# A transformer block and a retention, Fourier and convolution block: the order of the first tiles and weight slices, the norms' root, the norms in front of the feed-forward part by pairs, and an end by tiles

## The chip, the cores and the metric

One core of a Trainium2 chip runs the whole program, in one launch, float32 in and out. The metric is the device time in microseconds, the median of several executions; an execution's profile adds a span (first to last instruction of the program) and the clock granted to TensorE. The engines are PE (TensorE; PEld is its loading of stationary tiles), DVE (VectorE), ACT (ScalarE), POOL (GpSimd) and SP (SyncE, which here only issues DMAs).

## The reference

Two blocks follow each other on x (1024 tokens of width 1024). The first has two layers of attention over 16 meta tokens and the sequence, in 8 groups of two heads; the second one layer with a token mixer and a feed-forward part:

```python
for l in range(2):                               # first block
    proj = rmsnorm(h, norm_gain[l]) @ w_in[l]    # q, k, v, gates, forget
    ...
    h = h + concat(do, fo) @ w_out[l]
x = rmsnorm(h, final_gain)[:, 16:]
h_lat = modulate(rms_norm(x, g_mix_pre), sh_a, sc_a)          # second block
mix = token_mixer(h_lat, w_in, w_out, ...)       # retention | Fourier
x = x + gt_a * rms_norm(mix, g_mix_post)
h_ffn = modulate(rms_norm(x, g_ffn_pre), sh_f, sc_f)
u = conv3(h_ffn @ w_up)                          # 2 * 2816 columns
x = x + gt_f * rms_norm((silu(u_a) * u_b) @ w_down, g_ffn_post)
```

Every rms norm is x / sqrt(mean(x * x) + 1e-6) over a row.

## The kernel before

**Products.** A matrix product is three matmuls (`mm3`, L559): each operand is split into a high part rounded to fp32r and the rest, AH and AL for activations, WH and WL for weights, and high*high, high*low and low*high are added up in PSUM, a bank of 512 columns each. The activations of a stage stand transposed in AH and AL, 8 tiles of 128 rows. Weights come in slices of 512 KB: SP loads slice w into one of two slots of W32 (L2328) once the slice two before it is split; ACT writes WH (L1103) once PE is done with the slice two before (`W_OVER`); DVE writes WL (L1567). `split_to(w)` does all slices up to w at that place of an engine's program.

**Order.** Each engine has one program in order, written out by hand; counting semaphores (`mark` and `at`) tie them together. PSUM banks are planned ahead: `banks.take` gives the bank that was taken longest ago and names what its user before has to have finished, and PE waits for that.

**A norm** works on pairs of token tiles (`PAIRS`; the fifth has the 16 meta rows; for the first block `PAIR_ORDER` begins with it). ACT squares each tile with a sum into a column (L1115), DVE scales the sums by 1/1024 and adds 1e-6 (`mean`, L1573), ACT takes Ln (L1117) and Exp of -0.5 times it (L1119), DVE multiplies the tiles by it (L1602; L1883 between the blocks; L2132 in front of the feed-forward part), PE transposes them (L568, 16 transposes a pair over 8 banks), and the result is written to AH and AL: in the first block by ACT (L1150) and DVE (L1610); between the blocks by ACT into one of two buffers (L1337), POOL into AH (L2288) and DVE into AL (L1889); in front of the feed-forward part, 512 columns at a time, by ACT (L1134) and DVE twice (L1589, L1591).

**Start.** SP loads constants, the meta rows, then the 8 tiles of x with the first two weight slices behind the fourth and the sixth (L2330 to L2341). ACT's order is: statistics of the meta rows, of pair 0, fill of the meta rows, statistics of pair 1, fill of pair 0, statistics of pair 2, splits of the slices for q and k, fill of pair 1, statistics of pair 3. PE then does chunks of the first projection (352 or 344 tokens, 24 matmuls): q 0, fill of pair 2, k 0, fill of pair 3, q 1, q 2, k 1, k 2.

**Between the blocks** each pair of the last layer is added (L1840), normed by the final gain (L1875, stored to xs by POOL), normed once more and filled, while PE begins the context's product, whose 512-column results ACT evicts (L1354).

**In front of the feed-forward part.** The product `out2` runs in quarters of 256 columns: for the first three all tiles with the first weight slice and then the second, in the last pair by pair. ACT (L1461) and DVE (L2119) evict two pairs each into MX. When all are there, for four tiles at a time: squares, root, product with the root and the gate row GA (L2125), add of XL (L2128), squares again, root, scaling (L2132). XL has room for four tiles; POOL reloads each when its add is done (L2309) and stores the sum to xs (L2310). Then all is transposed and filled, and only when the last fill is done does the up projection begin: 22 blocks of 128 columns, for each the halves a and b, for each two chunks of 512 tokens, with a convolution on ACT (L1485) and DVE (L2149, L2152) behind each.

**End.** The down projection runs in two halves of 512 columns, for each k of 22 all eight tiles (eight banks). ACT (L1513) and DVE (L2176) evict. Behind the last matmul DVE makes the gate row (L2068), and four tiles at a time ACT squares both halves (L1522, L1523), takes Ln and Exp (L1526, L1528), DVE multiplies (L2189) and adds (L2192), and POOL stores each tile (L2320); SP waits for the stores.

## Time and profile before

| what | value |
|---|---|
| time, median of 3 runs | 3196.71 us (3195.51 to 3205.25) |
| profiled execution | 3192.36 us, span 3190.6 us |
| mean granted clock of TensorE | 0.952 of 2.4 GHz |
| busy PE, DVE, ACT, POOL | 2850.3, 1543.7, 1058.5, 170.3 us |
| moved by DMA | 198.06 MB, mean 62 GB/s |

A row of a group of instructions has its line, engine, operation, what it writes and reads with the shapes, the count, then busy time, mean ns of one, and the idle time of the engine ahead of them with what ended it. A window's row has the busy time of each engine in that stretch (number of instructions in brackets) and the granted clock as a share: 1.00 is 2.4 GHz, 0.50 is 1.2 GHz. In a timeline the first two numbers are start and duration; brackets hold idle time ahead and the releaser.

### The profile page before, as it was taken

The numbers are of one execution on the slowest core, as the hardware profiler recorded it, in microseconds if no ns is written. First come the engines' busy times: TensorE is split into PE (matmuls) and PEld (weight loads), VectorE is DVE, ScalarE is ACT, GpSimd is POOL, SyncE is SP. The second block draws the span as 40 slices with busy tenths as digits, with TensorE's granted clock in tenths as the row PEclk, the third lists the DMA queues.
The fourth block names the chain that finished last, engine by engine and source line by source line (L and its number), as shares of the span: only waits on it lengthen the run. The fifth ranks groups of instructions, "written<-read, shape, count | busy, mean of one in ns | idle before, by whom it ended". The sixth has DMA issues, their size and how long they took to land.

```text
span 3190.6 us, 42795 instructions
## 1 busy us (share of the span) xinstructions
PE 2850.3 (89%) x17412; PEld 2434.0 (76%) x17412; DVE 1543.7 (48%) x2759; ACT 1058.5 (33%) x1867; POOL 170.3 (5%) x263
## 2 busy tenths in 40 slices
PE   5889999999789899999997969999948999999994
PEld 5777777887778777787886857888937888887883
DVE  4555654545335555555454355553244444444334
ACT  6333333333143233332233371223243222223222
POOL 1000000000001011000001020000000000000000
PEclk9899999999899999999998879999979999999997
DMA  5212221211321221222213131112221111111121
GB/s 121 39 52 60 62 54 55 62 41 41 114 86 31 50 62 56 54 65 65 59 47 112 39 123 36 40 53 98 73 93 41 47 47 47 52 47 40 53 104 62
DMA packets 205393, 198.06 MB, mean 62 GB/s; under 512 B 7286, under 2 KB 181686, under 8 KB 205198
## 3 DMA queue, kind: packets, MB, share of 16 engines
q1 hardware_dynamic: 186192, 130.07, 15.8%
q0 software_dynamic: 19008, 65.26, 5.5%
q8 instruction: 140, 2.29, 0.3%
q14 instruction: 53, 0.43, 0.0%
HBM read 162.73 MB, written 32.58 MB: 61 GB/s over the span
## 4 chain that ended last, share of the span: by engine, by line
PE 77%; DVE 9%; ACT 6%; issue 4%; DMA 3%; POOL 0%; SPq 0%; ACTq 0%; DVEq 0%; POOLq 0%
PE PS L559 73%; PE PS L568 4%; DMA W<-in_w_in 2%; DVE WL L1567 1%; DVE ST L1744 1%; ACT WH L1103 1%; ACT top L1242 1%; DMA TMP<-s_os 1%; ACT L1117 1%; DVE AL L1610 1%; ACT OTt L1115 0%; ACT R L1115 0%; DVE AL L1591 0%; DVE V L1732 0%; DVE R L2189 0%
## 5 line engine op out<-in xcount | busy, mean ns | idle before, releaser
L559 PE MATMUL PS<-AH,WH 128*128 128x344 f32 (+2 forms) x2608 | 991.6, 380 | 37.0 <-DVE AL L1610 21.4
L559 PE MATMUL PS<-AL,WH 128*128 128x344 f32 (+2 forms) x2608 | 921.0, 353 | 0.0
L559 PE MATMUL PS<-AH,WL 128*128 128x344 f32 (+2 forms) x2608 | 918.4, 352 | 0.0
L559 PEld LDWEIGHTS PS<-AH,WH 128*128 128x128 f32 x2608 | 498.0, 191 | 120.0 <-DVE AL L1610 23.0
L559 PEld LDWEIGHTS PS<-AL,WH 128*128 128x128 f32 x2608 | 499.0, 191 | 50.5 <-issue 1.4
L559 PEld LDWEIGHTS PS<-AH,WL 128*128 128x128 f32 x2608 | 497.0, 191 | 44.0
L1567 DVE TENSOR_TENSOR WL<-W,WH 128x1024 fp32r<-128x1024 f32 x188 | 230.0, 1226 | 398.6 <-ACT WH L1103 398.2
L559 PE MATMUL PS<-WH,AH 128*128 128x256 f32 (+1 forms) x1152 | 369.4, 321 | 15.1 <-DVE AL L2171 7.2
L559 PE MATMUL PS<-WL,AH 128*128 128x256 f32 (+1 forms) x1152 | 368.1, 320 | 0.0
L559 PE MATMUL PS<-WH,AL 128*128 128x256 f32 (+1 forms) x1152 | 368.0, 319 | 0.0
L1103 ACT ACTIVATE WH<-W 128x1024 fp32r<-128x1024 f32 x188 | 197.3, 1051 | 348.8 <-PE PS L559 322.8
L1744 DVE TENSOR_REDUCE ST<-PS 128x1 f32<-128x784 f32 (+8 forms) x272 | 188.0, 732 | 150.4 <-PE PS L559 150.0
L568 PE MATMUL PS<-ident,top 128*128 128x128 f32 (+2 forms) x1132 | 190.1, 284 | 71.9 <-issue 20.6
L559 PEld LDWEIGHTS PS<-WH,AH 128*128 128x128 f32 x1152 | 222.1, 193 | 33.3 <-DVE AL L2171 7.7
L559 PEld LDWEIGHTS PS<-WH,AL 128*128 128x128 f32 x1152 | 222.1, 193 | 15.3
L559 PEld LDWEIGHTS PS<-WL,AH 128*128 128x128 f32 x1152 | 221.9, 193 | 15.2
L1242 ACT ACTIVATE top<-PS,ST 128x784 f32<-128x784 f32 (+8 forms) x272 | 194.2, 721 | 90.4 <-DVE ST L1744 58.2
L568 PEld LDWEIGHTS PS<-ident,top 128*128 128x128 f32 (+2 forms) x1132 | 134.0, 136 | 106.3 <-issue 42.1
L559 PE MATMUL PS<-top,V 128*64 128x256 f32 (+6 forms) x1176 | 185.7, 378 | 19.9 <-DVE top L1781 17.1
L559 PEld LDWEIGHTS PS<-top,V 128*64 128x64 f32 (+3 forms) x1176 | 120.5, 156 | 88.0 <-issue 43.4
L1485 ACT ACTIVATE R<-PS,R 128x512 f32<-128x512 f32 x88 | 68.6, 780 | 321.4 <-PE PS L559 321.4
L2149 DVE SCALAR_TENSOR_TENSOR R<-PS,R 128x504 f32<-128x504 f32 x88 | 65.4, 743 | 208.7 <-ACT R L1485 208.7
(300 smaller groups left out, 3163.9 us busy)
## 6 DMA issues: line engine op xcount, KB each, us to landing
W<-in_w_in SPq DMA_DIRECT2D x94, 512.0 KB, 7.4
W<-in_w_ada SPq DMA_DIRECT2D x48, 512.0 KB, 3.6
W<-in_w_up SPq DMA_DIRECT2D x44, 512.0 KB, 3.7
W<-in_w_out SPq DMA_DIRECT2D x24, 512.0 KB, 3.4
W<-in_w_down SPq DMA_DIRECT2D x22, 512.0 KB, 3.6
R<-s_xs POOLq DMA_DIRECT2D x16, 512.0 KB, 6.0
s_adap<-AST POOLq DMA_DIRECT2D x48, 128.0 KB, 7.4
top<-in_x SPq DMA_DIRECT2D x8, 512.0 KB, 9.6
```

The costliest lines, as they stand in the source:

```text
L559: return e.matmul(out, lhsT, rhs, start=start, stop=stop, skip_group_check=True)
L568: return e.transpose(out, in_, ident[0:k, 0:k])
L1103: e.activation(WH[:, t, :], W32[:, s, :], ACT.Copy).then_inc(*w_hi.mark(v))
L1117: e.activation(cols[0:r, :], cols[0:r, :], ACT.Ln).then_inc(*logged.mark(tag))
L1242: e.activation(P[0:rows, P_SLOT[u], 0:W], PSf[0:rows, o:o + W], ACT.Exp, bias=st[:, 0:1], accum_out=st[:, 1:2]).then_inc(*exped.mark(u))
L1485: e.activation(dst[:, c:c + n], bank(b), ACT.Identity, scale=CW[:, 1, jj:jj + 1], bias=CW[:, 3, jj:jj + 1]).then_inc(*conv_a.mark((j, ab, ...
L1567: e.tensor_tensor(WL[:, t, :], W32[:, s, :], f(WH[:, t, :]), ALU.subtract).then_inc(*w_lo.mark(v))
L1610: e.scalar_tensor_tensor(lo, bank(b)[:, 0:n], COLS[:, 8 * l + k:8 * l + k + 1], f(hi), ALU.mult, ALU.subtract).then_inc(*fill_lo.mark((l, ...
L1744: e.tensor_reduce(ST[0:rows, ST_SLOT[u], 0:1], PSf[0:rows, o:o + W], AX.X, ALU.max, negate=True).then_inc(*row_max.mark(u))
L2149: e.scalar_tensor_tensor(d3[:, :, 1:64], o3[:, :, 0:63], CW[:, 0, jj:jj + 1], d3[:, :, 1:64], ALU.mult, ALU.add).then_inc(*conv_v.mark((j, ...
```

## The change

- **Root.** `mean`, Ln and Exp become ACT's Sqrt with scale 1/1024 and a bias column EPS, and DVE's reciprocal, in all norms but that of the retention.
- **Start.** For the first layer ACT and DVE do: statistics of the meta rows, of pair 0, fill, statistics of pair 1, fill, split of q's slice, fill of pair 1, statistics of pair 2, split of k's slice. PE's chunks are q 0, fill of pair 2 (then statistics of pair 3 on ACT and DVE), k 0, q 1, fill of pair 3, k 1, q 2, k 2; the constants' set-up stands ahead of q 2.
- **In front of the feed-forward part.** Each quarter of `out2` is squared by ACT from PSUM, 256 columns at a time into SQ, and written to MX by DVE already multiplied by the gate row. Root, add and second norm go by pairs, the first two beside the last quarter. The fill of pair 0 stands on PE between the third and the fourth pair of that quarter, that of pair 1 behind it, those of pairs 2 and 3 between the first chunks of the up projection, which for the first block goes a 0, b 0, a 1, b 1. ACT fills 256 columns into one of four buffers, POOL writes AH, DVE AL.
- **End.** In the second half the last four k go tile by tile. ACT squares the first half during the second, and DVE multiplies it by the gate row, made ahead; of each tile of the second half the bank itself is squared and multiplied, one root a tile, one product with the root and add over 1024 columns. SP issues the stores.
- **Besides.** The load of the convolution's constants stands ahead of the Fourier part; stores of two tiles share a semaphore.

The diff, cut to its core:

```diff
@@ statistics (ACT) and its DVE part
-                e.wait_ge(*mean_sq.at(tag))
-                e.activation(cols[0:r, :], cols[0:r, :], ACT.Ln).then_inc(*logged.mark(tag))
-                e.wait_ge(*logged.at(tag))
-                e.activation(cols[0:r, :], cols[0:r, :], ACT.Exp, scale=-0.5).then_inc(*rstd.mark(tag))
+                e.wait_ge(*squared.at((tag, len(tiles) - 1)))
+                e.activation(cols[0:r, :], cols[0:r, :], ACT.Sqrt, scale=1.0 / D, bias=EPS[0:r, :]).then_inc(*root.mark(tag))
...
-                e.tensor_scalar(cols[0:r, :], cols[0:r, :], 1.0 / D, 1e-6, ALU.mult, ALU.add).then_inc(*mean_sq.mark(tag))
+                e.wait_ge(*root.at(tag))
+                e.reciprocal(cols[0:r, :], cols[0:r, :]).then_inc(*rstd.mark(tag))
@@ scalar(e), norm
+                if l == 0:
+                    norm_stats(0, 4)
+                    norm_stats(0, 0)
+                    norm_fill(0, 4)
+                    norm_stats(0, 1)
+                    norm_fill(0, 0)
+                    split_to(WI[0, 0, "q"])
+                    norm_fill(0, 1)
+                    norm_stats(0, 2)
+                    split_to(WI[0, 0, "k"])
+                    return
@@ tensor_fourier and tensor_ffn
-            tensor_out(e, "out2", [128 * t for t in range(8)], first, lambda q, p: (mix_act if p % 2 else mix_dve, (q, p)))
+            tensor_out(e, "out2", [128 * t for t in range(8)], first, lambda q, p: (mix_dve, (q, p)),
+                       after=lambda i, among: tensor_norm_fill(e, "ffn", 0, among) if i == 2 else None)
+            tensor_norm_fill(e, "ffn", 1)
...
+                for ab, ci in UP_ORDER[j]:
+                    c, n = CH2[ci]
+                    if j == 0 and ab == 0:
+                        e.wait_ge(*fill_lo.at(("ffn", 2 * ci + 1, 7)))
+                    tensor_chunk(e, WI["up", j, ab], ("up", j, ab, ci), c, n, [(conv_v, (j, ab, ci))], ALL, ci == 1)
+                    if j == 0 and ci == 0:
+                        tensor_norm_fill(e, "ffn", 2 + ab, [b for b in ALL if b != banks.place["up", 0, ab, 0]])
...
+                together = FT - 4 * half
+                for k in range(together):
+                    for t in range(8):
+                        product(t, k)
+                for t in range(8):
+                    for k in range(together, FT):
+                        product(t, k)
@@ scalar(e), behind out2 (DVE: sum, add and scale of a pair at the same places)
+                mix_squares(3, 0)
+                mix_root(0)
+                sum_stats(0)
+                mix_squares(3, 1)
+                mix_root(1)
+                mix_squares(3, 2)
+                sum_stats(1)
+                mix_root(2)
+                ffn_fill(0)
+                mix_squares(3, 3)
+                split_to(WI["up", 0, 0])
+                ffn_fill(1)
+                split_to(WI["up", 0, 1])
+                sum_stats(2)
+                mix_root(3)
+                sum_stats(3)
+                ffn_fill(2)
@@ vector(e), the end
+                for t in range(8):
+                    r = RSTD[:, t:t + 1]
+                    e.wait_ge(*end_sq.at((t, 1)))
+                    e.tensor_tensor(r, r, RSTD[:, 8 + t:9 + t], ALU.add).then_inc(*end_v.mark(("sum", t)))
+                    e.tensor_tensor(G[:, t, 512:1024], bank(banks.place.get(("down", 1, t), 0)), GAf[:, 512:1024], ALU.mult).then_inc(
+                        *end_v.mark(("second", t)))
+                    inverse(("end", t), r)
+                    e.wait_ge(*rstd.at(("end", t)))
+                    e.wait_ge(*end_v.at(("second", t)))
+                    e.wait_ge(*tile_in[t].at("res"))
+                    e.scalar_tensor_tensor(XLf[:, t, :], G[:, t, :], r, XLf[:, t, :], ALU.mult, ALU.add).then_inc(*end_v.mark(("add", t)))
```

## Rows read from the trace of the kernel before

**Rows 1.** Page of the kernel before, busy time (share of the span)
```profile
PE 2850.3 (89%) x17412; PEld 2434.0 (76%) x17412; DVE 1543.7 (48%) x2759; ACT 1058.5 (33%) x1867; POOL 170.3 (5%) x263
```

**Rows 2.** Waits of PE, whole span: us in total, times, longest
```profile
PE PS L568 <- DVE R L2132: 41.7, 6, 26.0
...
PE PS L559 <- ACT R L1337: 16.5, 4, 14.5
```

**Rows 3.** Windows: us; busy PE, PEld, DVE, ACT, POOL; clock; DMA share; GB/s
```profile
0.00:37.62 37.62, 8.20 (x40) 7.04 (x40) 16.40 (x39) 31.93 (x61) 1.44 (x6) 0.87 0.87 209
...
1841.00:1863.05 22.05, 3.82 (x19) 3.31 (x17) 10.05 (x14) 20.60 (x32) 3.08 (x6) 0.57 0.27 112
...
2243.20:2334.60 91.40, 91.32 (x769) 90.88 (x767) 18.87 (x23) 13.33 (x17) 2.08 (x4) 1.00 0.19 64
...
2334.60:2401.60 67.00, 14.77 (x65) 10.68 (x65) 44.59 (x63) 44.42 (x67) 6.34 (x12) 0.58 0.29 102
...
3146.90:3190.60 43.70, 0.00 (x0) 0.00 (x0) 23.56 (x38) 17.12 (x41) 4.26 (x8) 0.55 0.24 96
```

**Rows 4.** Timeline, first 40 us: start us, us, engine, line, operation
```profile
8.84 0.20 ACT L1117 ACTIVATE SM<-SM 16x1 f32<-16x1 f32 x1
...
27.70 1.28 ACT L1117 ACT_TABLE_LOAD   x1
...
29.22 1.28 ACT L1119 ACT_TABLE_LOAD   x1
...
34.35 3.22 DVE L1610 SCALAR_TENSOR_TENSOR AL<-PS,COLS,AH 128x256 fp32r<-128x256 f32 x8
...
37.62 0.66 PE L559 MATMUL PS<-AH,WH 128*128 128x352 f32 x1 [9.60 <-DVE AL L1610]
```

**Rows 5.** Line L2328 (loads of W), its issue at 7.6 us
```profile
DMA to landing us min/median/max: 21.9/21.9/21.9
```

**Rows 6.** Windows at a gap of PE, columns as in rows 3
```profile
920.70:923.80 3.10, 0.00 (x1) 0.01 (x1) 1.62 (x4) 2.42 (x8) 0.96 (x2) 0.78 0.65 260
...
922.50:929.30 6.80, 5.50 (x26) 5.47 (x27) 2.32 (x10) 4.54 (x11) 0.00 (x0) 0.50 0.28 109
```

**Rows 7.** Timeline, norm of the second layer (ACT)
```profile
933.20 0.20 ACT L1117 ACTIVATE SM<-SM 128x2 f32<-128x2 f32 x1 [5.07 <-DVE SM L1573]
```

**Rows 8.** Timeline, between the blocks (ACT, DVE)
```profile
1875.52 0.58 ACT L1354 ACTIVATE R<-PS 128x512 f32<-128x512 f32 x1
...
1861.72 2.55 DVE L1567 TENSOR_TENSOR WL<-W,WH 128x1024 fp32r<-128x1024 f32 x2
```

**Rows 9.** Groups, 2334.6 to 2401.6 us: count, busy us, mean ns, idle
```profile
L1115 ACT ACTIVATE R<-R 128x1024 f32<-128x1024 f32 x16 | 16.9, 1056 | 14.7 <-DVE R L2128 13.1 <-DVE R L2119 0.9
...
L2125 DVE SCALAR_TENSOR_TENSOR R<-R,SM 128x1024 f32<-128x1024 f32 x8 | 10.2, 1280 | 5.7 <-ACT SM L1119 5.7
...
L2132 DVE TENSOR_SCALAR R<-R,SM 128x1024 f32<-128x1024 f32 x8 | 5.5, 748 | 5.7 <-ACT SM L1119 5.7
```

**Rows 10.** Groups by form, 1841 to 1905 us
```profile
L1337 ACT ACTIVATE R<-PS,COLS,SM 128x256 f32<-128x256 f32 x29 | 15.5, 561 | 11.0 <-DVE AL L1889 11.0
```

**Rows 11.** Windows: transposes alone, then matmuls; columns as in rows 3
```profile
2366.30:2369.70 3.40, 1.43 (x13) 1.19 (x11) 2.08 (x2) 1.24 (x2) 0.00 (x0) 1.00 0.00 0
...
2401.60:2407.30 5.70, 5.70 (x14) 4.50 (x15) 1.23 (x1) 1.06 (x1) 0.55 (x1) 0.50 0.05 16
```

**Rows 12.** Timeline, last weight slice (ACT, DVE)
```profile
3124.77 1.06 ACT L1103 ACTIVATE WH<-W 128x1024 fp32r<-128x1024 f32 x1 [8.13 <-PE PS L559]
...
3127.01 1.22 DVE L2171 TENSOR_TENSOR AL<-R,AH 128x1024 fp32r<-128x1024 f32 x1
```

**Rows 13.** Groups, 3124.7 to 3190.6 us
```profile
L1522 ACT ACTIVATE R<-R 128x512 f32<-128x512 f32 x8 | 5.0, 628 | 1.5 <-DVE R L2068 0.9
```

**Rows 14.** DMA issues from 3150 us: KB each, us to landing
```profile
out<-R POOLq DMA_DIRECT2D x8, 512.0 KB, 2.9
```

**Rows 15.** Sequencers at the end: ns min/median/max, start us
```profile
L96 POOLq DRAIN  x1: 8466/8466/8466, 3181.9 to 3181.9; - x1
```

More of the change, by code:

```diff
@@ L530, in build @@
         out_mm, out_added = count("out_mm"), count("out_added")
-        tile_out = [count(f"tile_out{i}") for i in range(8)]
+        tile_out = [count(f"tile_out{i}") for i in range(4)]
         fg_in, xc_in, fg_mul = count("fg_in"), [count(f"xc_in{i}") for i in range(2)], count("fg_mul")
@@ new lines, in fourier, with mix_root, sum_stats @@
+                    for p in range(4 if q < 3 else 0):
+                        mix_squares(q, p)
+                def mix_root(p):
+                    e.wait_ge(*mix_v.at(("sum", p)))
+                    r = RSTD[:, 2 * p:2 * p + 2]
+                    e.activation(r, r, ACT.Sqrt, scale=1.0 / D, bias=EPS).then_inc(*root.mark(("mix", p)))
+                def sum_stats(p):
+                    statistics(("mix2", p), [MX[:, t, :] for t in PAIRS[p]], lambda i: [(mix_v, ("add", PAIRS[p][i]))], RSTD[:, 8 + 2 * p:10 + 2 * p], JF)
@@ new lines, in ffn @@
+                        if half and 1 <= k <= 8:
+                            t = k - 1
+                            e.wait_ge(*(down_act if t % 2 else down_dve).at(t))
+                            if t:
+                                e.wait_ge(*end_sq.at((t - 1, 0)))
+                            e.activation(Jf[:, 0:512], F_OUT[t], ACT.Square, accum_out=RSTD[:, t:t + 1]).then_inc(*end_sq.mark((t, 0)))
+                    if half == 0:
+                        for t in range(1, 8, 2):
+                            b = banks.place.get(("down", 0, t), 0)
+                            e.wait_ge(*down_mm.at((0, FT - 1, t)))
+                            e.activation(F_OUT[t], bank(b), ACT.Copy).then_inc(*down_act.mark(t))
@@ new lines, in ffn @@
+                for t in range(8):
+                    e.wait_ge(*down_mm.at((1, FT - 1, t)))
+                    if t:
+                        e.wait_ge(*end_sq.at((t - 1, 1)))
+                    e.activation(Jf[:, 512:1024], bank(banks.place.get(("down", 1, t), 0)), ACT.Square, accum_out=RSTD[:, 8 + t:9 + t]).then_inc(
+                        *end_sq.mark((t, 1)))
+                    e.wait_ge(*end_v.at(("sum", t)))
+                    r = RSTD[:, t:t + 1]
+                    e.activation(r, r, ACT.Sqrt, scale=1.0 / D, bias=EPS).then_inc(*root.mark(("end", t)))
```

369 lines of the change are left out of this document (204 added, 165 removed).

## The prediction, made before the changed kernel ran

> **What bounds the kernel now.** The page comes first: PE is busy 2850.3 of the span's 3190.6 us [rows 1], so a change that touches no matmul can win back at most the 340 us in which PE stands still. Then PE's waits [rows 2]: the longest single ones are 26.0 us for L2132 (tiles scaled in front of the feed-forward part) and 14.5 us between the blocks. Then windows by stage [rows 3], which show where the idle time lies: 29.4 us ahead of the first projection (8.20 busy of 37.62), 18.2 between the blocks, 52.2 in front of the feed-forward part, and all 43.7 us behind the last matmul, 143.5 together. In each, ACT and DVE are busy by turns: the stages are chains, and what leaves the chain leaves the span. The window from 2243.2 to 2334.6 shows the opposite, a stage that PE fills (91.32 of 91.40).
>
> **Root and reciprocal in place of Ln and Exp.** For each pair of tiles ACT loads a table for Ln and another for Exp, 1.28 us each [rows 4]. Square and Copy load none in between, so they need no table of their own. With Sqrt alone the table stays: a pair's link shrinks from two loads, two ACTIVATEs of 0.20 us [rows 7] and a DVE step before them to one ACTIVATE with a DVE reciprocal behind it. I take the reciprocal of a few columns at 0.2 us, like those small steps; its bounds are 0.1 and the 0.75 of a whole tile's step [rows 9]. A pair saves 2.7 us of ACT. The Trainium skill (ScalarE: Activation LUTs, "Table sets: the hidden batching unit") says that one set holds both exp and ln, and that sqrt is in another; by that rule the exchange would save no load and add some, and -112 below would be about -70. The rows show a load ahead of each of the two, so they decide.
>
> **Start, -12.4.** PE's first chunk waits for the fill of the second pair, 37.57 [rows 4]. Before, ACT reads the third pair's statistics ahead of the split and that fill; now they stand behind (5.4 us), and the three links that stay ahead are 2.7 shorter (the 16-row tile's 1.5). Counted through: the first Ln stood at 8.84 [rows 4], and Sqrt stands there now and ends at 9.0; two squares (1.06 each [rows 9], and 0.2 each to read the sum, taken like a small ACTIVATE) and the root end at 11.7; 16-row fill and second pair's root at 15.6; 3.0 us of fill, 18.6; split of q, 19.6; second fill, 22.5. DVE follows with a scaling, a fill of 3.22 [rows 4], a split of 1.2 and another fill, and ends at 25.1: -12.4. The chunk for k needs the second slice, issued at 7.6 and landing 21.9 us later [rows 5], at 29.5; split it is ready at 31.8, and the chunk is due at 34.5, 9.4 after the first as before. So this load is barely in time: 3 us later and each further one is paid. Bounds -8 and -14.
>
> **Second layer's norm, -6.** Sqrt no longer stands behind DVE's add of the next pair; ACT waited 5.07 us there [rows 7]. Three links from add to fill are 1.6 us shorter (one load and its ACTIVATE): 4.8. The first follows a PE gap of 3.1 us, after which the granted clock was 0.50 (1.2 GHz) for 6.8 us with 5.50 of work [rows 6]; with a gap of 1.5 it may stay at 2.4 GHz, which is worth 2.5, and I count half. Bounds -3 and -8.
>
> **Between the blocks, -18.3.** The product ends at 1841.2 and DVE's add of its last pair at 1841.9. Then DVE has two products of 1.28, two scalings of 0.75, two products of 1.28 [rows 9] and three reciprocals, 7.2, and ACT's statistics (2.65 a pair, not 5.3) are in time for each. So its split starts at 1849.1 in place of 1861.72 [rows 8]: I take -12.9, with the load of DVE's queue at the first add. Further on ACT sets the pace: the eviction at 1875.52 [rows 8] stands behind two table loads, as does the next slice's: 2.7, twice. Bounds -13 and -21.
>
> **In front of the feed-forward part, -40.6.** ACT's and DVE's work on the first three pairs slides under the last quarter of the product, where PE takes 5.7 us a pair (91.40 for 16) [rows 3], so pairs end at 2317.5, 2323.2, 2328.9. Squares of 256 columns and the product with the gate row, both straight from PSUM, are new forms: I take 0.6 with the read and 0.7 us, nearest to the 0.63 of 512 columns [rows 13]; bounds 0.4 and 1.3 [rows 9]. A pair's handling, 2 us, stays under its 2.8 of PE. First pair: added until 2323.3, root 2324.8, scaled 2326.4. Second: added 2330.4, root 2333.1. PE's in-order fill of the first pair starts at 2328.9, but its last transposes wait for a bank that ACT frees only behind the second pair's root, at 2333.9. So the fourth pair's product, part of it at half clock, ends at 2342.8, not 2334.6. Its handling holds a bank of the second fill until 2345.0; ACT's split and 8 fills of 0.56 [rows 10] and DVE's behind them end at 2350.2, where the first chunk starts; it takes 8.3 us (14 of 24 matmuls in 5.7 at 1.2 GHz [rows 11], the rest at 0.23). Beside it the third and fourth pairs are squared, added and scaled until 2360.7; third fill and second chunk end at 2366.0, the fourth fill on DVE at 2371.3. There the third chunk starts and loses 2.7 to the clock: it counts as from 2374.0. Before, it began at 2415.4, two chunks (8.3 and 5.6) behind 2401.6: -41.4. Against it, the slice for the second half of the last quarter is split behind two squares and an eviction: +0.8. Bounds: -47 with full clock, -30 with all at half.
>
> **Tail, -35.0.** In the last half the final four k go tile by tile, so seven of eight tiles finish under PE (12 matmuls of 0.23, 2.77 us a tile). A tile needs ACT 0.63 and two small steps [rows 13], DVE 0.2, 0.7, 0.2 and 1.28 [rows 9], 2.4: they keep up. Behind the last matmul: square 0.8, sum 0.2, product 0.7 (root beside it), reciprocal 0.2, last product 1.3, hops 0.3, store 3.5 (POOL's took 2.9 [rows 14], I add some for another queue), end 0.3: 7.3. New wait: the last slice can be split only when k 17 is through, at 3124.77; the fill behind it ends at 3128.2 [rows 12], 3.5 later, where PE in the new order wants it after 9 matmuls, 2.1: +1.4. POOL's DRAIN takes 8.47 us behind its last store [rows 15] and ends the span; with the stores on SP it can run early. Of 43.7 us 8.7 stay. Bounds -30, if a DRAIN still follows the end, and -37.
>
> **Covered.** Fewer semaphores; the load of the convolution's constants ahead of the Fourier part and the gate row's ahead of the end, three DMAs of POOL under stages that PE fills to 0.99 [rows 3]; uncovered they cost their issue, 2 us in all. Sqrt also brings a table load to four later places with Exp or Tanh, beside PE's matmuls; on the path they cost 5.
>
> **Sum.** -12.4 -6.0 -18.3 -40.6 -35.0 = -112.3. The profiled execution took 3192.4: 3080.1. The median shown, 3196.7, lies 4.3 above it, and its three runs spread by 10. I forecast 3083 for the median.
>
> **Rivals.** *The clock stays low.* Pauses of 2 to 3 us keep PE at 1.2 GHz through the norms and from 2334 to 2380: another 12 us, 3095. For it: 0.58 is that stage's mean clock now [rows 3]. Against: 2.4 GHz was granted in a window with transposes alone, and came 5.7 us into the matmuls [rows 11]. Chance 0.2. The Trainium skill (TensorE: Matmul & The Clock Gate, "Part 4: PE-mode transpose") says that transposes do not count as busy; by that rule the fills would hold the clock down, and 3095 is what it gives. The first window of rows 11 speaks against it. *Tables come back.* Were Square or Identity missing from Sqrt's table, each root would cost two loads again, and the change would not do what it says: start -7, norm -2, blocks -3, front -29, tail -24 (ACT 3.6 us a tile against PE's 2.8): 3128. Against: Square runs in Exp's table without a load. 0.06. *More overlap.* Full clock in every stage, a store of 3: 3070. 0.16. *Slower.* A denser kernel is granted less clock: each 1% of mean clock costs 28.5 us of busy PE, so from 4% on it passes the 112 gained, and 6% gives 3255. Rows 3 have 91 dense microseconds at 1.00 and low clock only in the patchy windows. 0.01.
>
> **Numbers.** The sum has 0.57, the rivals the rest. The range is 3064 to 3103: it takes in the clock's case and the fuller overlap and leaves out tables and slower. A measurement of this kernel can tell some 0.3%, 10 us, from no change. Faster 0.98, same 0.01, slower 0.01.
>
> **What would show it.** Right: the first chunk at 25 us; no table load from 12 to 40 us; the first chunk between the blocks 9 us behind the product, not 22; no PE gap over 4 us in front of the feed-forward part; the last store issued by SP 4 us behind the last matmul. Wrong: PE's k chunk waiting for the second slice, a table load at every root, a PE wait of over 3 us at the last slice.

## The result, and the profile after

The changed kernel takes 3099.7 us (median of 4 runs, 3097.1 to 3102.0), the kernel before 3198.1 in the same series: a ratio of 0.969 [0.967, 0.971], 98.4 us less. The forecast was 3083 with a range of 3064 to 3103: the time lies inside, near its upper end, 16.7 above the forecast.

The profiled execution took 3101.8 with a span of 3099.8, 90.8 less than the span of before. First the page's busy times of the changed kernel, which answer to [rows 1]:

```profile
PE 2859.0 (92%) x17412; PEld 2438.5 (79%) x17412; DVE 1538.9 (50%) x2768; ACT 1011.7 (33%) x1865; POOL 183.2 (6%) x287
```

PE has the same 17412 matmuls and 8.7 us more of busy time; what left the span is idle time, 340.3 then and 240.8 now. ACT lost 46.8 us: 39 table loads of 1.28 us fewer are 50, and its other work grew by 3.

Windows by stage of the changed kernel, columns as in [rows 3]: until the first chunk; the rest of the first projections; between the blocks, from the product's end to the first chunk; 87.5 us of the out-projection that ends in front of the feed-forward part; from the fourth pair's product to the first up chunk; its first four chunks; behind the last matmul.

```profile
0.00:25.06 25.06, 7.75 (x41) 5.82 (x41) 13.74 (x36) 19.27 (x45) 1.43 (x6) 0.99 0.94 204
25.06:67.79 42.73, 36.05 (x194) 33.62 (x195) 22.39 (x50) 19.65 (x43) 5.59 (x5) 0.89 0.36 92
1835.80:1842.73 6.93, 0.01 (x1) 0.03 (x1) 6.86 (x10) 4.42 (x9) 2.69 (x5) 0.84 0.52 214
2221.50:2309.00 87.50, 86.57 (x732) 86.13 (x730) 31.68 (x43) 28.78 (x79) 5.86 (x12) 1.00 0.28 91
2312.90:2326.86 13.96, 9.22 (x61) 8.64 (x61) 12.51 (x23) 9.41 (x19) 8.25 (x16) 0.74 0.48 175
2326.86:2371.46 44.60, 32.87 (x128) 26.20 (x129) 20.44 (x33) 18.61 (x34) 9.54 (x18) 0.79 0.10 36
3093.85:3099.80 5.95, 0.00 (x1) 0.00 (x0) 2.24 (x5) 0.98 (x3) 0.00 (x0) 0.73 0.44 176
```

Beside [rows 3] the reader sees three things. The pause between the blocks is 6.93 us and has DVE at work for 6.86 of them: one engine is left in that chain, where ACT filled 20.6 of 22.05 before. In the out-projection PE is still full (86.57 of 87.50, at clock 1.00) while ACT has 28.8 us of work and DVE 31.7, where they had 13.3 and 18.9: this is the norm that slid under the product. And the window of the four chunks has PE idle for 11.7 us at a clock of 0.79. The first of its two pauses was not foreseen.

To see where each microsecond went, the two traces are cut at the same matmul, counted from the start of each (the 41st is the first chunk's; where the order differs, both orders have done the same amount); stages in us:

| stage (ends at matmul no.) | before | after | difference | forecast |
|---|---|---|---|---|
| to the first chunk (41) | 37.62 | 25.06 | -12.6 | -12.4 |
| first projections (234) | 38.02 | 42.73 | +4.7 | 0 |
| attention, first layer (5001) | 754.5 | 756.3 | +1.8 | 0 |
| norm of the second layer (5881) | 122.3 | 117.4 | -4.9 | -6.0 |
| attention, second layer (10501) | 724.5 | 728.8 | +4.3 | 0 |
| between the blocks (11904) | 260.8 | 245.4 | -15.4 | -18.3 |
| second block (14013) | 376.7 | 377.1 | +0.4 | 0 |
| in front of the feed-forward part (14341) | 112.1 | 78.7 | -33.4 | -40.6 |
| feed-forward part to the last matmul (17412) | 719.9 | 722.0 | +2.1 | +1.4 |
| end | 44.1 | 6.4 | -37.7 | -36.4 |

They sum to -90.8 against -112.3. Three places hold the difference: the first projections, attention stretches whose code did not change, and the stage in front of the feed-forward part.

Timeline of the changed kernel's start: the one table load for the root, the first chunks for q and k, DVE's scaling of the last pair, the set-up's table load and the matmul behind it (in brackets the engine's idle time and what ended it).

```profile
7.84 1.28 ACT L1144 ACT_TABLE_LOAD   x1
...
25.06 0.66 PE L569 MATMUL PS<-AH,WH 128*128 128x352 f32 x1 [3.83 <-DVE AL L1681]
...
34.37 0.43 PE L569 MATMUL PS<-AH,WH 128*128 128x352 f32 x1 [2.10 <-DVE AL L1681]
...
36.81 2.10 DVE L1673 TENSOR_SCALAR top<-top,SM 128x1024 f32<-128x1024 f32 x2
...
55.62 1.28 ACT L1214 ACT_TABLE_LOAD   x1
...
61.51 0.83 PE L569 MATMUL PS<-TMP,rotm 128*128 128x344 f32 x2 [2.78 <-ACT TMP L1254]
```

The first chunk starts at 25.06 and the one for k at 34.37; 25.1 and 34.5 stood in the working. Then the load at 55.62, for the Exp of the set-up, keeps ACT from the eviction that the rope product waits for, and PE stands still for 2.78 us at 61.51.

The same view in front of the feed-forward part, with DVE's fill (L2254) and its second convolution step (L2275):

```profile
2326.86 0.79 PE L569 MATMUL PS<-AH,WH 128*128 128x512 f32 x1 [2.85 <-DVE AL L2254]
...
2336.82 4.12 DVE L2254 TENSOR_TENSOR AL<-R,AH 128x256 fp32r<-128x256 f32 x8 [0.29 <-POOL AH L2444]
...
2341.63 0.74 DVE L2275 SCALAR_TENSOR_TENSOR R<-PS,R 128x504 f32<-128x504 f32 x1
...
2342.43 0.79 PE L569 MATMUL PS<-AH,WH 128*128 128x512 f32 x1 [5.63 <-DVE R L2275]
...
2356.50 0.74 DVE L2275 SCALAR_TENSOR_TENSOR R<-PS,R 128x504 f32<-128x504 f32 x1
...
2357.35 0.77 PE L569 MATMUL PS<-AH,WH 128*128 128x512 f32 x1 [5.85 <-issue]
```

The first up chunk starts at 2326.86. The second one's weights and data are there, and yet it starts 5.63 us after the transposes in front of it, directly behind L2275 at 2341.63. That is the convolution of the first chunk, which reads the first chunk's bank: the bank taken is the one taken longest ago, and that is the first chunk's own. DVE's convolution in turn stands in its queue behind eight steps of the third fill. The third chunk waits in the same way for the second's convolution at 2356.50; its own fill was through at 2355.8, so there the bank costs 1.4 of the 5.85.

The end of the changed kernel: PE at the last slice of weights, then the work of the last tile behind the last matmul (3093.85), and the stores.

```profile
3072.38 0.47 PE L569 MATMUL PS<-WH,AH 128*128 128x512 f32 x1 [1.11 <-DVE WL L1638]
...
3093.89 0.60 ACT L1596 ACTIVATE R<-PS 128x512 f32<-128x512 f32 x1 [1.57 <-PE PS L569]
...
3094.69 0.69 DVE L2312 TENSOR_TENSOR R<-PS,R 128x512 f32<-128x512 f32 x1
...
3094.80 0.29 ACT L1600 ACTIVATE SM<-SM 128x1 f32<-128x1 f32 x1 [0.23 <-DVE SM L2311]
...
3095.29 0.15 DVE L1644 RECIPROCAL SM<-SM 128x1 f32<-128x1 f32 x1
...
3095.48 1.28 DVE L2318 SCALAR_TENSOR_TENSOR R<-R,SM 128x1024 f32<-128x1024 f32 x1
```

```profile
out<-R SPq DMA_DIRECT2D x7, 512.0 KB, 2.6
```

PE waits 1.11 us at the last slice. Behind the last matmul: square 0.6, sum, gate product 0.69, reciprocal 0.15, last product 1.28, store 2.6; 5.95 in all.

### The profile page after: what moved, and what is told of

Same layout as the page of the kernel before. It is cut to its first block, busy times and chain, and to the rows that moved or that the text cites. A ratio compares the mean times of both kernels' runs of the same rounds, so it can differ in the third digit from the quotient of the medians.

```text
span 3099.8 us, 42844 instructions
## 1 busy us (share of the span) xinstructions
PE 2859.0 (92%) x17412; PEld 2438.5 (79%) x17412; DVE 1538.9 (50%) x2768; ACT 1011.7 (33%) x1865; POOL 183.2 (6%) x287
## 3 DMA queue, kind: packets, MB, share of 16 engines
q1 hardware_dynamic: 187344, 134.27, 16.6%
## 4 chain that ended last, share of the span: by engine, by line
PE 79%; DVE 9%; ACT 5%; issue 4%; DMA 3%; POOL 0%; SPq 0%; ACTq 0%; DVEq 0%; POOLq 0%
PE PS L569 75%; PE PS L578 4%; DMA W<-in_w_in 2%; DVE ST L1825 1%; DVE WL L1638 1%; ACT WH L1130 1%; ACT top L1278 1%; DMA TMP<-s_os 1%; DVE AL L2254 0%; DVE AL L1681 0%; DVE V L1813 0%; DVE top L1841 0%; DVE top L1838 0%; DVE AL L1900 0%; ACT AH L1316 0%
## 5 line engine op out<-in xcount | busy, mean ns | idle before, releaser
L569 PE MATMUL PS<-WH,AH 128*128 128x256 f32 (+1 forms) x1152 | 370.6, 322 | 16.7 <-DVE WL L1638 7.3
L569 PEld LDWEIGHTS PS<-WH,AH 128*128 128x128 f32 x1152 | 223.0, 194 | 35.7 <-DVE AL L2294 8.2
L1278 ACT ACTIVATE top<-PS,ST 128x784 f32<-128x784 f32 (+8 forms) x272 | 194.2, 720 | 90.6 <-DVE ST L1825 58.3
```

Of the source, the lines that this page charges most:

```text
L569: return e.matmul(out, lhsT, rhs, start=start, stop=stop, skip_group_check=True)
L1278: e.activation(P[0:rows, P_SLOT[u], 0:W], PSf[0:rows, o:o + W], ACT.Exp, bias=st[:, 0:1], accum_out=st[:, 1:2]).then_inc(*exped.mark(u))
```

## Experiments

All are the changed kernel with the edit shown, unless said otherwise; "..." marks lines of an edit that are left out. "Stage" is one of the table above. The span of one profile has up to 10 us of noise of its own (after_again shows it), so a stage is compared where the edit acts, and the medians for the whole. The changed kernel's own median was 3099.7 at first and 3097.2 when it ran once more. The differences of medians below are counted from 3099.7 and are uncertain by these 2.5 us.

**banks_free.** The second chunk may not take the first's bank, nor the third the second's.

```diff
-                    tensor_chunk(e, WI["up", j, ab], ("up", j, ab, ci), c, n, [(conv_v, (j, ab, ci))], ALL, ci == 1)
+                    late = {(0, 0, 1, 0): (0, 0), (0, 0, 0, 1): (1, 0)}.get((0, j, ab, ci))
+                    among = [b for b in ALL if late is None or b != banks.place["up", 0, late[0], late[1]]]
+                    tensor_chunk(e, WI["up", j, ab], ("up", j, ab, ci), c, n, [(conv_v, (j, ab, ci))], among, ci == 1)
```

> The changed kernel with one difference: of the first four chunks of the feed-forward part, the second may not take the bank of the first, nor the third that of the second, so neither has to wait for a convolution that DVE does behind eight steps of a fill. Theory 'bank': the 5.63 us gap at 2336.80 and most of the 5.85 us gap at 2351.50 in the changed kernel are waits for those banks; the second chunk then starts straight behind the transposes of the third fill, 5.5 us earlier and at the 2.4 GHz clock (another 2.7), the third chunk still waits for the last fill on ACT and DVE but for no convolution behind it (1.4 less), and the first part of the down product starts 8 to 10 us earlier, near 2837 instead of 2846; in all -7 to -10 us. Rival 'data': the second chunk waits for its weights or for the fill on DVE as well; the gap shrinks by at most 1.5 us and the time stays within 2 us.

Measured 3090.2 (3088.3 to 3093.9), 0.967 [0.965, 0.968] of before. The stage in front of the feed-forward part went from 78.7 to 68.0 us. PE's rows of that run with a wait:

```profile
2324.54 0.80 PE L569 MATMUL PS<-AH,WH 128*128 128x512 f32 x1 [2.89 <-DVE AL L2256]
...
2346.14 0.50 PE L569 MATMUL PS<-AH,WH 128*128 128x512 f32 x1 [3.99 <-DVE AL L2256]
```

Between the first chunk and the third (no. 14293) there is no pause for a bank; the third chunk waits only for its fill (L2256 is the fill's line here). Theory "bank" holds: the two waits and the half clock behind the first cost 10.7 us of that stage by these two profiles. The other profiles give this size its bounds: the seven with the banks as changed have the stage at 77.4 to 78.7 us, the three with the banks free (both and stats_later too) at 68.0 to 69.0. So the cost is 8.5 to 10.7 us.

**fills_first.** All four pairs filled ahead of the first chunk, chunks in their old order; everything else in front of the feed-forward part as changed.

```diff
-            tensor_norm_fill(e, "ffn", 1)
+            for p in (1, 2, 3):
+                tensor_norm_fill(e, "ffn", p)
...
-                    if j == 0 and ci == 0:
-                        tensor_norm_fill(e, "ffn", 2 + ab, [b for b in ALL if b != banks.place["up", 0, ab, 0]])
...
-        UP_ORDER = [[(0, 0), (1, 0), (0, 1), (1, 1)] if j == 0 else [(0, 0), (0, 1), (1, 0), (1, 1)] for j in range(FT)]
+        UP_ORDER = [[(0, 0), (0, 1), (1, 0), (1, 1)] for j in range(FT)]
```

> The changed kernel without the mixing of chunks and fills: all four pairs are filled ahead of the first chunk of the feed-forward part, and the chunks go in their old order; pairs, squares from PSUM and roots stay. Theory 'the banks eat it': in the changed kernel the third chunk starts at 2357.35; with the fills first, the third pair's fill ends on DVE at 2341, the fourth's at 2345.5, the first chunk starts there, and the third at 2345.5 + 8.3 + 5.6 = 2359.4. So mixing is worth only 2 to 3 us as it stands, and 12 with the banks free. Rival 'the mixing is the gain': the time rises by 8 us or more.

Measured 3093.0 (3089.8 to 3093.4), 0.967 [0.965, 0.968]; the stage takes 70.3 us, 8.4 less than as changed. (ACT and DVE do the last fill ahead of their first convolution.) Both readings put down beforehand missed the sign. The rows of PE in that run show why:

```profile
2329.48 3.65 PE L578 MATMUL PS<-ident,R 128*128 128x128 f32 x16 [6.49 <-DVE R L2219]
...
2335.42 3.43 PE L578 MATMUL PS<-ident,R 128*128 128x128 f32 x16 [2.29 <-ACT R L1540]
...
2338.76 0.76 PE L569 MATMUL PS<-AH,WH 128*128 128x512 f32 x1
```

I had let the first chunk wait for the last fill on DVE. It needs only the first two pairs, so it starts straight behind PE's last transposes, at 2338.76, and its 6.5 us cover the rest of the last fill on ACT and DVE. From there PE has no pause. So of the 33.4 us gained in this stage none comes from mixing chunks and fills: that part costs 8.4 as it stands. With the banks free it is worth 1.4 to 2.3 by the stage (69.0 to 68.0 against 70.3), which the medians, 3093.0 and 3090.2 with overlapping ranges, cannot tell from nothing.

**exp_early.** One Exp of one column behind the last pair's root, where ACT is idle.

```diff
                 def step_stats(p):
                     norm_stats(l, p)
+                    e.activation(SM[:, 63:64], EPS, ACT.Exp)
```

> The changed kernel with one ACTIVATE more: an Exp of one column right behind the root of the last pair of tiles at 36.3 us, where ACT is idle until 40.0. Theory 'late table': of the 4.7 us that the start gives back between 46 and 62 us, 1.3 is the table load of the set-up's Exp at 55.62, and the rest the lower clock behind the longer pause of 2.78 us; with the load moved, that pause shrinks to 1.5 or less, the clock stays, and the start keeps 10.5 to 12 us at 62 us instead of 7.9: -2 to -4 us. Rival 'place': the set-up stands in ACT's queue ahead of the eviction whatever its table, 2.9 us of copies and small steps that stood two chunks later before; then at most 1.3 us comes back.

Measured 3097.1 (3091.8 to 3100.2), 0.969 [0.967, 0.970]. In the profile the load moved under ACT's idle time and PE's pause is half as long:

```profile
37.67 1.28 ACT L1320 ACT_TABLE_LOAD   x1
...
60.51 0.82 PE L569 MATMUL PS<-TMP,rotm 128*128 128x344 f32 x2 [1.40 <-ACT TMP L1254]
```

The first projections take 41.2 us in place of 42.7 (1.5 back, of the 4.7 lost); the median is inside the noise of the changed kernel. That the 1.5 us are real is told by all profiles with the changed start and its roots: the six without the early Exp end this stage at 67.2 to 68.5 us, the three with it (exp_early, both, stats_later) at 65.5 to 66.3. The result lies between the two readings: the pause of 2.78 us is one of 1.40, and 8.9 us are kept at the eviction behind the set-up (60.51 against 69.36 before), not 10.5. The rest of the loss is ahead of it: at matmul 113 (a rope product, at 41.76 us in the changed kernel) only 10.5 of the 12.6 us are left. No run tells what takes those 2.1 us.

**start_as_before.** The start's order of before, with roots.

```diff
             def norm(l):
-                if l == 0:
-                    norm_stats(0, 4)
...
-                    split_to(WI[0, 0, "q"])
-                    norm_fill(0, 1)
-                    norm_stats(0, 2)
-                    split_to(WI[0, 0, "k"])
-                    return
                 for i, p in enumerate(PAIR_ORDER):
```

(DVE's order and the order of the first projections go back in the same way.)

> The changed kernel with the start's order of before (three pairs' statistics ahead of the first slice's split, the first projections in their old order) and everything else as changed, roots included. It tells what of the 12.6 us at the first chunk is the order and what is the roots in place of Ln and Exp. My steps: two pairs and the 16-row tile at 2.7, 2.7 and 1.5 us less of tables each would bring the first chunk to 37.6 - 6.9 = 30.7 us or so, the order the remaining 5.4; so +5 us at the first chunk, and at 62 us +1 to +5, since the set-up with its table load then lies elsewhere. Rival 'loads': the first chunk waits for the loads of x and of the weights anyway, and the order is worth under 1 us.

Measured 3109.2 (3108.1 to 3111.6), 0.973 [0.971, 0.974]: 9.5 slower than as changed.

```profile
30.08 1.06 ACT L1127 ACTIVATE WH<-W 128x1024 fp32r<-128x1024 f32 x1 [6.72 <-DMA W<-in_w_in]
...
35.59 0.66 PE L566 MATMUL PS<-AH,WH 128*128 128x352 f32 x1 [14.40 <-DVE AL L1667]
...
75.25 1.49 PE L566 MATMUL PS<-TMP,rotm 128*128 128x344 f32 x2 [2.80 <-ACT TMP L1240]
```

The first chunk stands at 35.59: the roots alone bring 2.0 of the 12.6 us, where I had 6.9. The first row says why. In the old order ACT splits the slices for q and for k ahead of the second pair's fill, and with the shorter links it gets there so early that it stands idle for 6.72 us until the slice for k has landed. And at matmul 234 this kernel is at 75.95, the kernel before at 75.65: what the roots bring is lost again by then, and the pause behind the set-up is the longer one (2.80 at 75.25). So rival "loads" falls in its price, for the order is worth 10.5 us at the first chunk and not under 1, but not in its mechanism: some 6 of the 10.5 are one load of weights taken out of the first chunk's way (ACT waits 6.72 us for it, and DVE 5.97 behind ACT).

**ln_exp_norms.** Ln and Exp, with DVE's scaling in front, back in all norms but the two new ones.

```diff
-                e.activation(cols[0:r, :], cols[0:r, :], ACT.Sqrt, scale=1.0 / D, bias=EPS[0:r, :]).then_inc(*root.mark(tag))
...
+                e.wait_ge(*mean_sq.at(tag))
+                e.activation(cols[0:r, :], cols[0:r, :], ACT.Ln).then_inc(*logged.mark(tag))
+                e.wait_ge(*logged.at(tag))
+                e.activation(cols[0:r, :], cols[0:r, :], ACT.Exp, scale=-0.5).then_inc(*rstd.mark(tag))
...
-                inverse((l, p), RSTD[:, t0:t0 + n], r)
+                mean((l, p), n, RSTD[:, t0:t0 + n], r)
```

> The changed kernel with Ln and Exp, and DVE's scaling ahead of them, back in the norms of the two layers, of the context, between the blocks and of the latent tiles; the roots stay in front of the feed-forward part and in the end. Theory 'tables': the start's first chunk goes from 25.1 to 31 to 33 us (three links of 2.7, 2.7 and 1.5, some of it hidden by DVE), the second layer's norm gives back 4 to 6 us, the stage between the blocks 15 to 18: in all +24 to +32 us. Rival 'order': the gain comes from the order of the steps, and the tables return at no more than half of that, +8 to +15. Rival 'clock': a table less in the attention between them moves nothing, the norms' gains are partly eaten by lower clock in the attention, and the sum is smaller than the stages' own, +18 to +24.

Measured 3132.6 (3130.7 to 3136.6), 0.980 [0.979, 0.982]: 32.9 slower by the medians, 28.7 by the spans: theory "tables" (24 to 32) holds, and neither rival does. PE's first chunk, and its first behind the product between the blocks:

```profile
31.66 0.66 PE L570 MATMUL PS<-AH,WH 128*128 128x352 f32 x1 [3.27 <-DVE AL L1693]
...
1870.90 0.55 PE L570 MATMUL PS<-WH,KH 128*128 128x256 f32 x1 [14.88 <-ACT R L1383]
```

The first chunk is 6.6 us later than as changed. With start_as_before that gives the start from both sides: order alone 6.0 (37.62 to 31.66), the roots on top of it 6.6, both 12.6; but the roots alone 2.0, since without the order ACT then waits for the slice for k. The stages give back 4.7 (norm of the second layer) and 15.3 (between the blocks: 260.75 us, before 260.83). So the whole gain of these two stages is the exchange. It has two parts that no run separates: the table loads, and DVE's scaling step with its wait, which stood between squares and Ln.

**stores_by_pool** and **before_sp_stores.** The result's stores moved to the other issuer, in the changed kernel and in the kernel before.

```diff
                 e.dma_start(XLf[:, t, :], xs[128 * t:128 * t + 128, :]).then_inc(*tile_in[t].landed("res"))
+            for t in range(8):
+                e.wait_ge(*end_v.at(("add", t)))
+                e.dma_start(O["out"][0][128 * t:128 * t + 128, :], XLf[:, t, :]).then_inc(*out_done.landed("all" if t == 7 else t))
...
-            for t in range(8):
-                e.wait_ge(*end_v.at(("add", t)))
-                e.dma_start(O["out"][0][128 * t:128 * t + 128, :], XLf[:, t, :]).then_inc(*out_done.landed("all" if t == 7 else t))
```

> The changed kernel with the eight stores of the result issued by POOL, as before the change, instead of SP. Theory 'drain': the DRAIN of 8.47 us that followed POOL's last store before the change belongs to a queue that still has stores of its own in hand; it comes back, and the time between the last matmul and the end goes from 5.95 us to some 16 to 18: +9 to +13 us. Rival 'store': POOL only needs somewhat longer to issue and land a store than SP, and the tail grows by 1 to 3 us.

> The kernel before with only the issuer of the result's eight stores changed, from POOL to SP; its untiled end stays. Theory 'drain': POOL's DRAIN runs long before the end, and the 43.7 us behind the last matmul shrink by the DRAIN's 8.47 us to 34 to 36, the span by 8 to 10. Rival 'store': the last add of DVE sets the end, a store by SP takes as long as one by POOL with its drain, and less than 3 us are gained.

Measured 3106.6 (3104.7 to 3111.8), 6.9 slower than as changed; and 3192.5 (3190.0 to 3199.5), a ratio of 0.998 [0.997, 0.999] to before. Behind the last matmul POOL's stores make 11.85 us of the changed kernel's 5.95, and SP's stores make 37.8 of 43.7 in the kernel before: 5.9 and 6.0. The row of POOL's DRAIN in stores_by_pool, in ns, with its start:

```profile
L96 POOLq DRAIN  x1: 8472/8472/8472, 3094.1 to 3094.1; - x1
```

and in before_sp_stores, where it starts far from the end:

```profile
L96 POOLq DRAIN  x1: 18221/18221/18221, 3104.8 to 3104.8; - x1
```

The DRAIN returns with its 8.47 us, but it begins while the last store is under way, and SP's 2.6 us for that store go. So it costs 6, not 9 to 13 in the one kernel and 8 to 10 in the other. Behind POOL's last loads it lasts 18.2 us (17.5 as changed), and nobody waits for it.

**no_tiled_end.** All eight tiles at each step, to the end.

```diff
-                together = FT - 4 * half
+                together = FT
```

> The changed kernel with the last four steps of the down product's second half in the order of before, all eight tiles at each step, so that the tiles end 0.69 us apart and not 2.77; squares, gate and last product of each tile stay in their new form. Theory 'tiles under PE': the tail then is eight tiles of DVE at 2.3 us (0.16 + 0.69 + 0.15 + 1.28) less what lies under the last matmuls, 5.95 + 7 x (2.3 - 0.69) = 17.2 us; against it the wait at the last slice of weights (1.1 us and its clock, 1.5) goes: +9 to +11 us. Rival 'order is cheap': what the tail gained came from the smaller steps and the stores alone, and the time rises by less than 4 us.

Measured 3106.9 (3105.3 to 3109.9), 0.971 [0.969, 0.972], 7.2 slower than as changed (8.7 by the stages), under the 9 to 11 put down, but well over the rival's 4. DVE's last product, 12.2 us behind the last matmul (3091.45; in the changed kernel 1.6):

```profile
3103.62 1.28 DVE L2318 SCALAR_TENSOR_TENSOR R<-R,SM 128x1024 f32<-128x1024 f32 x1
```

DVE needs 2.06 us a tile where I had 2.3, the time behind the last matmul is 16.6, and 1.9 come back ahead of it, in the feed-forward stage (720.1 for 722.0). So of the 37.8 us that the change took from behind the last matmul (43.7 to 5.95) the order of the last four steps is worth 10.6, for 1.9 ahead of it, the stores by SP 5.9, and the rest is some 21. By subtraction that is the work that was made smaller or moved ahead (the first half's squares and gate products under the matmuls, one root with a bias in place of two tables, no evictions); no run takes these apart.

**both.** banks_free and exp_early together, and three tiles that pass two steps before the last slice is asked for.

```diff
+                first = 3 if half else 0
+                for t in range(first):
+                    for k in range(together, FT - 2):
+                        product(t, k)
                 for t in range(8):
-                    for k in range(together, FT):
+                    for k in range(FT - 2 if t < first else together, FT):
                         product(t, k)
```

> The changed kernel with three small differences together: the banks of the first chunks of the feed-forward part (-9.9 us in its own run's profile), the early Exp in the start (-1.7), and, new, the tiled end with the first three tiles passing two steps each before the last slice of weights is asked for, so that its split (2.4 us and the fill behind it) lies under 18 matmuls (4.2 us) instead of 6 (1.4). Theory 'each wait by itself': the gap of 1.11 us at the last slice goes and the tail stays within 1 us of 5.95, for -1 to -1.5; with the other two about -13, near 3087. Rival 'the tail slips': three tiles end closer together, DVE with 2.3 us a tile falls behind, and the tail grows by 1 to 3 us, for no gain at the end; about 3089.

Measured 3086.9 (3085.2 to 3089.8), a ratio of 0.965 [0.963, 0.966]: the shortest of all, 12.8 us under the changed kernel's median (10.3 under that of after_again). PE has no wait at the last slice, the feed-forward stage is 720.1 us (722.0), the end 5.95 as before it. "Each wait by itself" holds.

**stats_later.** both, with the last pair's statistics behind the first chunk for k: `+ chunk(0, "k", 0) + [("stats", 3)]`.

> The version with the free banks, the early Exp and the later last slice, and one more difference: the last pair's statistics and scaling go behind the first chunk for k, not ahead of its rope steps. Theory 'rope behind statistics': in the changed kernel DVE scales tiles from 36.8 to 38.8 while PE's first rope product waits for it, part of the 2.0 us that the start loses between its first chunk and 42 us; moved, it gives 0.5 to 1.5 us back, near 3086. Rival 'fill behind statistics': the fill of the last pair then comes later, the chunks for k and q behind it wait, and it costs 1 to 3 us.

Measured 3088.2 (3085.2 to 3089.2), 0.965 [0.964, 0.967]; the first projections take 41.15 us against 40.50 in both. Neither gain nor a loss that can be measured: where the statistics stand is not what is left of the start's loss. What is stays open.

**after_again.** The changed kernel once more, no edit.

> The changed kernel itself, once more, so that its time stands beside the versions of this series and a second profile tells what of its stages repeats. If the differences between the attention stretches of the two first profiles (layer 1: 754.5 before and 756.3 after, layer 2: 724.5 and 728.8, same instructions) come from the change, they stand here again within 0.5 us. If they are the granted clock behind pauses of the same length, they move by 1 to 3 us with no pattern. Start 67.8, norm 117.4, in front of the feed-forward part 78.7 and the end 6.4 should stand again within 0.5. Time 3099.7 within 2.

Measured 3097.2 (3091.2 to 3104.5), 0.969 [0.968, 0.970], with a profile of 3089.3 us, 10.5 below the first. The attention stretches are 754.7 and 723.7 us, not 756.3 and 728.8; the start 68.4, the norm 116.1, between the blocks 243.2, in front of the feed-forward part 77.7 and the end 6.3. So the attentions moved by 1.6 and 5.1 us with no edit; but the norm and the stage in front of the feed-forward part moved too, by 1.3 and 1.0, where I had allowed 0.5. The window behind one pause of the first layer, in the first profile:

```profile
738.00:741.40 3.40, 3.35 (x20) 3.11 (x20) 0.00 (x0) 0.00 (x0) 0.00 (x0) 0.50 0.42 141
```

and in the second, the same 3.4 us of the same program:

```profile
738.00:741.40 3.40, 3.40 (x31) 3.04 (x31) 1.30 (x2) 0.00 (x0) 0.00 (x0) 1.00 0.41 139
```

The pause ahead of it is 1.81 us in the one and 1.80 in the other (736.24 and 736.17 to 738.05 and 737.98). Once 1.2 GHz was granted for the next 3.4 us, with 20 matmuls begun, and once 2.4 GHz, with 31.

## Why the prediction came out as it did

**What bounds the kernel.** Right: no matmul changed, and 99.5 us of PE's idle time went, nearly all in the four stages named.

**Roots for Ln and Exp.** Right: no table load lies between the roots of a stage, and 42 are left of 81. The exchange is worth 33 us by ln_exp_norms. With Ln and Exp back there are 72 loads, one ahead of each Ln and each Exp in a norm. The Trainium skill's rule that one set holds exp and ln (ScalarE: Activation LUTs, "Table sets: the hidden batching unit"), by which the exchange saves no load, is not what this program shows. The new root with its bias took 0.30 us where I had 0.20, which changed nothing.

**Start, -12.4.** Right for the first chunk (25.06), for k (34.37) and for the load of its weights; and for its two parts, 5.4 for the order and 6.9 for the roots, where 6.0 and 6.6 were measured in that order. What it didn't see is that the second part needs the first: the roots alone bring 2.0, because the slice for k lands at 29.6 to 30.1 and stood in the way. The term failed in what it left out: it counted the first chunk as the whole stage, and 4.7 us are given back before matmul 234. 1.5 of them are the table load of the set-up's Exp with the pause that it lengthens. I had such loads as four "beside PE's matmuls" at a cost of nothing, 5 if on the path; the cover was missing there, because the eviction that PE waits for is queued behind it.

**Second layer's norm, -6.** -4.9 in one profile and -6.2 in the other, between the bounds.

**Between the blocks, -18.3.** -15.4 and -17.7. The first chunk came 13.6 earlier (12.9 in the working, whose own steps give 12.6) and the next two brought 5.2 (5.4). The 3.4 us lost after that in the first profile lie in a stretch with the same pauses of 0.57 and 1.00 us as before, at half clock for longer. Of the other nine profiles with the roots in this stage, four have the stage at 243.1 to 243.5 us and five, like the first, at 245.2 to 245.8.

**In front of the feed-forward part, -40.6.** This is the term that failed: -33.4 and -34.4. Counted on the changed kernel's clock (21.7 earlier at matmul 14013), the fourth pair's product was to end at 2321.1, the first up chunk to start at 2328.5, and they came at 2319.2 and 2326.9. Then the working has "third fill and second chunk end at 2366.0", that is the second chunk straight behind the first, and at 2366.0 - 21.7 = 2344.3 it should have been done; it started at 2342.43. The step said nothing of the bank that this chunk takes. I had followed the banks for the fills ("its last transposes wait for a bank") and not for the chunks, and the pause of 5.63 brought a half clock with it. With the banks free the stage is 68.0 to 69.0, 43.1 to 44.1 less than before: 2.5 to 3.5 more than forecast. So the working of the pairs, squares and fills stood, and the one wait left out cost 8.5 to 10.7 us. The pause ahead of the third chunk was mostly in the working (5.3 us between 2366.0 and 2371.3).

**Tail, -35.0.** -37.7 at the end and +2.1 ahead of it, together -35.7. The new wait at the last slice was seen (1.4 forecast; a wait of 1.11 us, 1.9 with what it brings, by no_tiled_end and both), as was POOL's DRAIN, whose share was sized at 8.5 and is 6. The store took 2.6, not 3.5, and the rest of the 7.3 was 3.4, not 3.8.

**Covered, 0.** The DMAs moved on POOL's queue show in no wait. Of the table loads one was not covered, above.

**The rivals.** "The clock stays low" forecast 3095, the nearest number. It occurred in part: from 2321.8 to 2362.8 PE had half clock for some 24 us in three stretches. The working had counted on it in the first chunk and at the third; the stretch in between, which it had not counted on, came with the wait for the bank. It is the first of these rows (columns as in [rows 3]); with the banks free there are only the two stretches of the other rows, 13.6 us together:

```profile
2338.90:2345.69 6.79, 3.26 (x8) 2.59 (x9) 3.44 (x7) 1.43 (x3) 1.43 (x3) 0.50 0.00 0
...
2319.40:2329.60 10.20, 7.31 (x24) 5.85 (x22) 8.21 (x15) 7.35 (x15) 4.08 (x8) 0.50 0.53 156
2346.70:2350.10 3.40, 3.40 (x9) 2.65 (x8) 0.79 (x2) 0.00 (x0) 0.00 (x0) 0.50 0.02 5
```

So the number was near for another reason than the one given, pauses of 2 to 3 us by themselves. The rival on tables had a sum that is 3 us too low: its stages give -65 and so 3127.4 for the profile, 3130 for the median. "Tables come back", "more overlap" and "slower" did not occur; the mean granted clock over the span rose from 0.952 to 0.963.

**The base of the sum.** The profiled execution of before, 3192.4, was a short one: the medians of that kernel were 3197.5 to 3200.3 over this series. I added 3 us for it where 5.7 were due; that of the changed kernel was 2.1 above its median. So the two profiles are 90.6 apart and the medians 98.4. The stages fall 21.5 us short of the sum: 7.2 in front of the feed-forward part, 4.5 in the start, 6.5 in the two attentions and the second block, 2.9 between the blocks, 1.1 in the norm, less 0.6 at the end. The first two are of the change, by the runs above. The third is the clock of single executions: after_again has the two attentions at 754.7 and 723.7 us, and before_sp_stores, with the kernel before there, has them at 756.2 and 727.7. Most of the fourth is clock too, by after_again, but it stands in six of ten profiles.

**How much of it was luck.** The time lies 3.3 us inside the range's upper end. That end was set for the clock's rival; it was used up by the wait for a bank and the start's loss, both at nothing in the sum and in no rival. The number is in the range in part by luck, while the terms for the start's first chunk, the norm, the blocks and the end hold one by one within their bounds.

**The signs.** Met: the first chunk at 25.06; no table load between 12 and 40 us (the nearest stand at 7.84 and 55.62); the first chunk between the blocks 6.9 us behind the product; the last store issued 2.9 us behind the last matmul. Not met: "no PE gap over 4 us in front of the feed-forward part", where 5.63 and 5.85 were measured, and the working had 5.3 itself. None of the signs of being wrong came.

## What to carry to other kernels

When steps of different engines are mixed by hand, follow every buffer that the mixed steps take, the product's own bank too: "the one taken longest ago" can be the worst choice behind a block of short-lived ones, since its reader may be queued behind all of them, as here. Count a stage to a point where both orders have done the same work, not to its first product; and try the plain order beside the mixed one, for here it was the faster until the banks were freed. When links get shorter, look again at what then comes last: here a load of weights ate most of what the roots bring, until the order kept it off the path. Where a table changes in front of a PE wait, look for an idle place of ACT just ahead and load it there with an instruction of one column; here that halved one pause.

## What was not expected of the hardware

The same pause, 1.81 and 1.80 us in two executions of one program, was followed by half clock in one and by full clock in the other; over the series the same instructions took 754.5 to 758.1 us in the first layer's attention and 723.7 to 730.9 in the second's. The spans of two profiles of the changed kernel lie 10.5 us apart, while its stages around the norms repeat within 0.6 to 2.3. POOL's DRAIN lasts 8.47 us where it follows its last store of the result, and 16.0 to 18.2 (eleven profiles) where it follows its last loads, 50 us and more before the end.
